# Splitting a first block's projections into high and low parts, with a new order of its stages

## The reference, cut to what matters

```python
# first block (hybrid_layer)
h = rms_norm(x, norm_g) * (1 + scale) + shift          # scale, shift, gate from silu(c) @ w_ada
proj = h @ w_in                                        # 1024 -> 2840 columns
q, kcr, vcr, ksl, vsl, kwn, vwn, z_a, g_br, u, z_s = split(proj)
q = rms_norm(q per head); k_slc, k_win likewise, then rope on q, k_slc, k_win
kc, vc = compress(kcr), compress(vcr)                  # gelu(blocks @ w1) @ w2
attn = nsa_attention(...) * silu(z_a)                  # compressed, selected and window branches
y = s5_mixer(u, ...)                                   # state space model, chunks of 8 tokens here
y = gelu(y); y = y * sigmoid(y @ glu_w + glu_b)
ssm = y * silu(z_s)
x = x + gate * (concat[attn, ssm] @ w_out)
# second block, two layers: rmsnorm, projections, two attentions, output projection (not changed)
```

## Time and profile before

| | us |
|---|---|
| median of 3 runs | 1032.58 (1031.73 to 1033.58) |
| profiled execution, its own time | 1031.98 |
| its span | 1030.1 |
| PE busy | 970.0 (94% of the span) |
| DVE busy | 578.7 (56%) |
| ACT busy | 428.1 (42%) |
| POOL busy | 86.3 (8%) |

### The profile page before, as it was taken

How to read it: one execution, slowest core, us unless ns; L and a number is a source line. 1 busy time by engine, 2 the same in 40 slices (tenths; PEclk the granted TensorE clock), 3 DMA queues, 4 the chain that set the end, 5 groups by cost and what they waited for, 6 DMA issues and landing times.

```text
span 1030.1 us, 13812 instructions
## 1 busy us (share of the span) xinstructions
PE 970.0 (94%) x5345; PEld 713.8 (69%) x5345; DVE 578.7 (56%) x1232; ACT 428.1 (42%) x936; POOL 86.3 (8%) x117
## 2 busy tenths in 40 slices
PE   3899999999898999999999998999999999998996
PEld 1446576744455677888678886788888678886784
DVE  2889499442589845533695244735333786234732
ACT  4221220123366733332592524833333592434821
POOL 1001310120008000000001000000000001000000
PEclk9899999999999999999899999999999899999998
DMA  9734157052460003343311533213333220433102
GB/s 361 280 116 92 54 76 245 1 164 82 163 165 1 2 21 106 121 126 100 93 59 42 143 92 97 101 54 111 97 103 100 80 98 24 126 100 123 63 1 82
DMA packets 81523, 104.64 MB, mean 102 GB/s; under 512 B 3745, under 2 KB 51921, under 8 KB 81442
## 3 DMA queue, kind: packets, MB, share of 16 engines
q1 hardware_dynamic: 75362, 81.24, 24.7%
q0 software_dynamic: 5808, 22.15, 7.8%
q10 hardware_dynamic: 288, 0.36, 0.1%
HBM read 98.37 MB, written 4.19 MB: 100 GB/s over the span
## 4 chain that ended last, share of the span: by engine, by line
PE 79%; DVE 8%; ACT 5%; DMA 3%; issue 3%; SPq 0%; DVEq 0%; POOL 0%; POOLq 0%; ACTq 0%; PEldq 0%
PE bank L883 74%; DVE ring L1781 2%; DMA ring<-in_w_in 2%; ACT ring L793 2%; PE bank L1130 1%; PE bank L1160 1%; DMA ring<-in_w_ada 1%; DMA ring<-in_cmp_w_v 1%; PE bank L1304 1%; DVE arena L1812 1%; DVE soft L1791 1%; DVE soft L1812 1%; ACT soft L800 1%; PE bank L1216 1%; ACT w_hi L743 0%
## 5 line engine op out<-in xcount | busy, mean ns | idle before, releaser
L1827 DVE TENSOR_TENSOR w_lo<-ring,w_hi 128x1024 fp32r<-128x1024 f32 x80 | 97.8, 1225 | 114.4 <-ACT w_hi L743 111.3
L883 PE MATMUL bank<-w_hi,hT_hi 128*128 128x512 f32 x320 | 125.3, 392 | 1.3 <-issue 1.0
L883 PE MATMUL bank<-hT_hi,w_hi 128*128 128x512 f32 x320 | 125.7, 393 | 0.0
L883 PE MATMUL bank<-w_lo,hT_hi 128*128 128x512 f32 x320 | 124.6, 389 | 0.0
L883 PE MATMUL bank<-hT_lo,w_hi 128*128 128x512 f32 x320 | 124.6, 389 | 0.0
L883 PE MATMUL bank<-hT_hi,w_lo 128*128 128x512 f32 x320 | 124.5, 389 | 0.0
L883 PE MATMUL bank<-w_hi,hT_lo 128*128 128x512 f32 x320 | 124.5, 389 | 0.0
L883 PE MATMUL bank<-hT_t,ring 128*128 128x512 f32 x224 | 100.1, 604 | 4.2 <-DMA ring<-in_w_in 3.6
L743 ACT ACTIVATE w_hi<-ring 128x1024 fp32r<-128x1024 f32 x80 | 84.4, 1058 | 11.6 <-PE bank L883 11.4
L883 PEld LDWEIGHTS bank<-hT_t,ring 128*128 128x128 f32 x224 | 42.5, 193 | 56.8 <-issue 53.1
L883 PEld LDWEIGHTS bank<-w_hi,hT_hi 128*128 128x128 f32 x320 | 60.1, 188 | 14.7 <-issue 2.6
(11 more groups left out here) (289 smaller groups left out, 1616.2 us busy)
## 6 DMA issues: line engine op xcount, KB each, us to landing
ring<-in_w_in SPq DMA_DIRECT2D x64, 512.0 KB, 4.5
ring<-in_w_ada SPq DMA_DIRECT2D x4, 2048.0 KB, 9.8
ring<-in_w_in SPq DMA_DIRECT2D x4, 2048.0 KB, 10.4
bias_ring<-in_na_bias POOLq DMA_DIRECT2D x8, 1024.0 KB, 5.3
ring<-in_w_out SPq DMA_DIRECT2D x16, 512.0 KB, 3.5
arena<-in_w_ada SPq DMA_DIRECT2D x2, 2048.0 KB, 19.4
ring<-in_w_out SPq DMA_DIRECT2D x2, 2048.0 KB, 13.1
bias_ring<-in_t_bias POOLq DMA_DIRECT2D x8, 448.0 KB, 3.7
```

Source lines behind the costliest of these rows:

```text
L883: return pe.matmul(out, lhsT, rhs, start=first, stop=last)
L1827: dve.tensor_tensor(w_lo[:, u % 4], raw_w[:, u % 4], w_hi[:, u % 4].bitcast(fp32), SUB).then_inc(S["w_split"], 1)
```

## The change

1. **Projections in three passes.** Every projection of the first block (U, KC, KV, KW, Q, ZS, ZA) becomes three float32r matmuls over high and low parts. `hT` is split into `x_hi` (ACT, 8 casts) and `hT_r` (DVE blocks 0 to 3, POOL blocks 4 to 7); DVE now applies scale and shift to all eight blocks. The weights are split in 24 parts: ACT makes every high part, DVE the low part 0, POOL the low parts 1 to 23. A part is 128x1024 (U, KC, ZS, ZA: one tile's weights; KV: half of them; Q: a quarter) or 128x560 (KW: a quarter).
2. **Order.** PE: U, KC, KV, KW, wt, kk, v, Q, W1, state products, ZS, ZA, GLU. DVE: after `cl_ready` the squares, scaling and turning of both kinds of keys for all four tiles at once (instructions of 512 and 256 elements), then the states, then queries two tiles at a time, then the hidden layer.
3. **Places and queues.** `toe` moves from `x_t` to three places and is filled by 24 DMAs; these and the DMAs of `u_dram` and `y_dram` are issued by SP between weight chunks. POOL zeroes the three places (one after `cl_ready`). `silu(z_a)` moves on DVE from the first turns of the pair loop to before the compressed softmax, and `ssm_out` moves four turns earlier. The first half of U's weights has a semaphore of its own.

```diff
+            def part_lo(n):                                   # POOL
+                pool.wait_ge(S["p_hi"], n + 1)
+                pool.tensor_tensor(p_lo(n), p_raw(n), p_hi(n).bitcast(fp32), SUB).then_inc(S["p_lo"], 1)
...
+            for k in range(4, KD):
+                pool.wait_ge(S["h_hi"], k + 1)
+                pool.tensor_tensor(hT_r[:, k, :], hT[:, k, :], x_hi[:, k, :].bitcast(fp32), SUB).then_inc(S["h_upper"], 1)
+            for n in range(1, 4):
+                part_lo(n)
+            settle(pool.memset(soft[:, 0:2048], 0.0))
+            settle(pool.memset(gate_b[:, :], 0.0))
+            for n in range(4, 12):
+                part_lo(n)
+            pool.wait_ge(S["cl_ready"], 1)
+            pool.memset(spent, 0.0).then_inc(S["zeroed"], 1)
+            part_lo(12)
+            pool.wait_ge(S["k_stats"], 1)
+            inv_root(HD, EPS, "k_rstd", lambda v: by_tile(v)[:, :, 8:12])
+            for n in range(13, 16):
+                part_lo(n)
+            for r in range(2):
+                pool.wait_ge(S["q_stats"], r + 1)
+                inv_root(HD, EPS, "q_rstd", lambda v: by_tile(v)[:, 2 * r:2 * r + 2, 0:8])
+            part_lo(16)
+            part_lo(17)
+            za_lo(0)
+            za_lo(1)
+            part_lo(18)
+            part_lo(19)
...
+            def proj_T(p, n):                                 # PE
                 if p >= 4:
                     pe.wait_ge(S["proj_evac"], p - 3)
+                part_ready(n)
+                for k in range(KD):
                     if p == 0:
                         pe.wait_ge(S["h_lower" if k < 4 else "h_upper"], k % 4 + 1)
+                    ins = mm3(bank[p % 4][:, :], (p_hi(n)[:, k, :], p_lo(n)[:, k, :]), (x_hi[:, k, :], hT_r[:, k, :]), k, k == 0, k == KD - 1)
...
+            for k in range(KD):                               # DVE
+                dve.tensor_scalar(hT[:, k, :], hT[:, k, :], modA[:, k:k + 1], modS[:, k:k + 1], MUL, ADD).then_inc(S["h_raw"], 1)
             for k in range(4):
-                dve.tensor_scalar(hT[:, k, :], ...).then_inc(S["h_lower"], 1)
+                if k == 1:
+                    dve.wait_ge(S["p_hi"], 1)
+                    dve.tensor_tensor(p_lo(0), p_raw(0), p_hi(0).bitcast(fp32), SUB).then_inc(S["u0_lo"], 1)
+                dve.wait_ge(S["h_hi"], k + 1)
+                dve.tensor_tensor(hT_r[:, k, :], hT[:, k, :], x_hi[:, k, :].bitcast(fp32), SUB).then_inc(S["h_lower"], 1)
...
+            for k in range(KD):                               # ACT
+                act.wait_ge(S["h_raw"], k + 1)
+                act.activation(x_hi[:, k, :], hT[:, k, :], ACT.Copy).then_inc(S["h_hi"], 1)
+                if k == 3:
+                    part_hi(0)
+            for n in range(1, 4):
+                part_hi(n)
             for f in range(4):
                 if f == 2:
                     act.wait_ge(S["ang_ready"], 1)
...
                 act.activation(cut(uT[:, f * T:(f + 1) * T], s=LC, n=NCH), src, ACT.Copy).then_inc(S["proj_evac"], 1)
+                part_hi(4 + f)
...
+                elif c == CH_W1:                              # SP
+                    sp.wait_ge(S["zeroed"], 2)
+                    sp.wait_ge(S["kk_evac"], 8)
+                    for g0, part in toe:
+                        for s in range(LC):
+                            sp.dma_start(part[s * SC:(s + 1) * SC, :, (LC - 1 - s) * SC:P],
+                                         kk[:, g0:g0 + part.shape[1], 0:(s + 1) * SC]).then_inc(S["toe_in"], 16)
```

More of the change, by code:

```diff
@@ L462, in _ @@
[L462 to L480, removed]
@@ L606, in _ @@
                 act.activation(q_tok[:, i, :], src[:, :], ACT.Copy).then_inc(S["proj_evac"], 1)
[L607 to L615, removed]
-                act.activation(dst, cut(bank[4 + n % 4][0:SC, :], a=4, m=P), ACT.Copy).then_inc(S["kk_evac"], 1)
             act.wait_ge(S["lam_dot"], 1)
             act.activation(lam_t, lam_t, ACT.Exp).then_inc(S["lam_exp"], 1)
-            for i in range(NT):
-                src = proj(PT_KW + i)
-                act.activation(kvw[:, i, :], src[:, 0:280], ACT.Copy).then_inc(S["proj_evac"], 1)
             for s in range(2):
@@ L624, in _ @@
                 act.activation(hid_tok[:, s * 256:(s + 1) * 256], bank[s][0:66, 0:256], ACT.Copy).then_inc(S["hid_evac"], 1)
+            part_hi(16)
+            part_hi(17)
+            for n in range(4):
+                act.wait_ge(S["y_done"], 4)
+                two, q = n % 2, n // 2
+                dst = u_in.rearrange("p (q a b) n -> p q a b n", q=2, b=2)[:, q, :, two, :]
+                act.activation(dst, cut(bank[4 + n][:, :], a=8, n=NCH), ACT.Copy).then_inc(S["y_evac"], 1)
+            za_hi(0)
+            za_hi(1)
             def move_zs(f):
@@ L1009, in _ @@
             ins.then_inc(S["hidT_done"], 1)
-            arrived(CH_ZS)
+            pe.wait_ge(S["toe_in"], 16 * LC * len(toe))
+            pe.wait_ge(S["state_ready"], 1)
+            st = cut(tmp_c, g=SG, n=NCH)
+            for n in range(4):
+                two, q = n % 2, n // 2
+                for a in range(8):
+                    g = 2 * (8 * q + a) + two
+                    w = NCH if a == 7 else 2 * NCH
+                    out = bank[4 + n][:, a * NCH:a * NCH + w]
+                    wide_ = lambda v: v.rearrange("p g n -> p (g n)")[:, g * NCH:g * NCH + w]
+                    mm(out, toe_of(g), wide_(u_in), True, False)
+                    ins = mm(out, cl3[:, g, SC:SC + P], wide_(st), False, True)
+                ins.then_inc(S["y_done"], 1)
             for f in range(4):
@@ L1014, in _ @@
                     pe.wait_ge(S["hid_ready"], 1)
[L1015 to L1031 removed]
+                proj_T(PT_ZS + f, 16 + f)
+                if f == 2:
                     pe.wait_ge(S["hid_gelu"], 1)
@@ L1217, in rows_T @@
                     ins.then_inc(S["xT_done"], 1)
-            def mm3(out, a, b, k, first, last):
-                mm(out, a[0], b[0], first, False)
-                mm(out, a[1], b[0], False, False)
-                return mm(out, a[0], b[1], False, last)
             def tile_T(out, l, g, f):
@@ new lines, in over_all, with squares, scale_heads @@
+            def over_all(v, n, h):
+                return v.unsqueeze(1).unsqueeze(1).to_broadcast([P, n, h, HD])
+            def squares(src, h, out, place):
+                sq = cut(place, i=src.shape[1], h=h, d=HD)
+                tt(sq, pairs_of(src, h), pairs_of(src, h), MUL)
+                return dve.tensor_reduce(out, sq, AX.X, ADD)
+            def scale_heads(src, h, r, g):
+                v = pairs_of(src, h)
+                tt(v, v, r.unsqueeze(3).to_broadcast([P, src.shape[1], h, HD]), MUL)
+                tt(v, v, over_all(row(g), src.shape[1], h), MUL)
```

410 lines of the change are left out of this document (243 added, 167 removed).

## The result

| | median us | runs | ratio to before, 95% interval |
|---|---|---|---|
| before | 1033.08 | 1031.73 to 1033.82 | |
| changed | 1051.92 | 1049.98 to 1053.0 | 1.0182 [1.0162, 1.0202] |

The change costs 19 us where 8 were forecast as a gain; the time is 10 us outside the range. The profiled execution has a span of 1048.2 us against 1030.1.

The account below looks back on a forecast made before the run. PE was taken to bound the kernel (79% of the chain). Its 33 us gain is waited away up to ZS's end; GLU 5.5 earlier plus pair loop 2.0 gives 7.5 off, median 1025.1 us, range 1011 to 1042.

Parts of the forecast that it names:

- Rows stand on both sides, so I take half.: DVE working beside POOL's low parts: it loses half of POOL's time, between a floor of nothing and all of it.
- rival A: DVE's two-input instructions wait for POOL's whole instruction, up to `cl_ready` and from `state_ready` to `hid_ready`: +16, 1040; chance 0.33.
- The row at 125.47: POOL's small scaling took 0.70 and ended just after DVE's two-input instruction; read as blocking in reverse.
- The scalings of the earlier trace: Two 128x384 DVE scalings took 2.49 us beside POOL's split of `w_out`, 0.87 after it; read as a full block.
- the toe blocks: `toe` filled after kk by 24 DMAs from SP: 15.4 us from kk's end kept, floor 10, ceiling 25.
- this rival: Low parts make PE wait tile by tile; dismissed as no rival, 2.37 us against 5.46, with no chance given.
- PE's gap ahead of kk: PE waits 18 us for `cl_ready` after wt, from 102.6 to 120.6.
- The clock behind a pause: PE's clock is low after the wait ahead of kk; kk takes 7.2 + 1.8 us.
- rival C: SP's 24 small DMAs for `toe` are slow, 10 us above the value taken: 1035; chance 0.07.
- The stall at ZS 2: PE at ZS tile 2 waits for `hid_ready`, which stands behind the queries on DVE: 2.9 us.
- PE's gain: Three float32r passes save 26.4 us on 18 tiles; with KV and KW, together 33 us.
- the halves: Half of POOL's time charged to DVE: 1.9, 6.5, 5, 2.4 and 5.9 us up to ZS tile 2.

Follow-up runs that it names:

- experiment 1: Changed kernel, but POOL makes none of the first block's low parts; PE takes the high part in their place: 1015.24 us, ratio 0.9817 to the kernel before.
- experiment 2: Kernel before with 16 idle 128x1024 POOL instructions, eight ahead of the u DMAs, eight behind: subtractions 1043.63 us, fills 1034.64, copies 1034.56.

## Why the prediction was wrong

**The step that failed: "Rows stand on both sides, so I take half."** DVE pays nearly all of POOL's 1.27 and 2.37 us, 0.87 by the two traces of experiment 1. By the prediction's own steps: the angles lose 16.7 us (6.5 taken, and 1.9 ahead of them, where DVE lost nothing); sines' end to `cl_ready`, 77.5 to 130.8, is 53.3 instead of 44.3, 9.0 of POOL's 10.3 (5 taken). `cl_ready` came at 130.8, forecast 120.6, rival A 131 to 134. From `state_ready` to `hid_ready` it took 36.2 us where 27.9 were written: six parts at 12.6 instead of five at 5.9, the rest a little more work of DVE's own.

The prediction weighed three rows and read one of them wrongly. DVE's instruction of 126.87 ran untouched inside POOL's 2.39 us root, but that root has 10 elements, so its length says nothing of how much it reads. It was no evidence on a subtraction that reads 1024 columns twice. It was not even a row without a clash: the same root took 1.95 us at 118.99, where DVE had next to nothing to do. The row at 125.47 has the new form on DVE's side alone, and there it was POOL that waited. The scalings of the earlier trace rows have it on POOL's side alone. No row had both, as the prediction says itself. Taking the mean of contrary rows was the error, as none of them measured the new work; experiment 2, sixteen idle subtractions in the kernel before, is what prices it.

The Trainium skill, page "SBUF — State Buffer", has GpSimd's reads, not its writes, contend with a two-input DVE instruction (section "Who interferes with whom"), and the later of the two block fully until the first ends (section "Summary: rules for kernel authors"). The subtractions (2.2 us lost of 2.37) and the fills (0 lost) agree; the copies (0.8 lost of 1.22) agree in kind and not in size. The prediction cited the rule and priced it as rival A, at 1040, and gave it 0.33; even that was 12 us short, for the reasons that follow.

**Where the late start of ZS tile 2 comes from.** It began at 223.0, forecast 202.1. Of these 20.9 us, 10.2 are `cl_ready`, 0.6 the clock behind kk's pause, 4.2 the toe blocks, and 8.3 the way from `state_ready` to `hid_ready`. The states gave 2.5 back: parts 14 and 15 fell at 152.0 and 157.6, where DVE was waiting for the toe blocks anyway, so they cost it nothing. Of the whole miss of 26.8 us this is most; the rest is named below.

**Further terms that were mis-sized.** The first tiles: KW and wt were to be done at 102.6 and were done at 112.7, since PE waited 4.3 us for low parts in U (the prediction dismissed this rival with 2.37 against 5.46, but POOL took 3.28 a part and four low blocks of `hT` came first) and ran at the lower clock around it (0.50 from 52 to 57). This is why PE's gap ahead of kk was 18.2, the forecast's 18, though both of its ends were 10 us late: one number that fits is no proof of the steps behind it. The clock behind a pause: kk lost 2.3, not 1.8; ZS 2 and 3 took 15.06 us where 12.2 was due, which had no term at all. The toe blocks: 19.6 us behind kk's evacuation, 15.4 taken, rival C's direction at less than half its size; the landing of 10.4 us in that sum was 2 on SP's queue, and the issues took 17.7 instead of 5. `state_ready` came at 186.8, forecast 174.2. The stall at ZS 2: 8.86, forecast 2.9.

**What held.** Float32r at 512 columns takes 0.232 us a matmul, at 256 0.118 and at 280 0.129, a little above the values taken (by these the 33 us of PE's gain are about 30, an estimate). The prediction's sums hold to within a microsecond: KW's end comes to 98.2 where it has 98.8, rival A's median to 1041 where it has 1040. The pair loop gave 1.5 of its 2.0: GLU is 19.0 later, the output projection 17.6 (403.94 against 386.39). The conditions for failure were named rightly: "if `state_ready` is past 185 the forecast is wrong at the halves". And with PE's 33 us less work and no low parts on POOL, experiment 1 came out 18.7 us faster than the kernel before.

## What to carry to other kernels

Before work goes to an engine that is 8% busy, look for which other engine it holds up: here POOL's 2.37 us cost DVE 2.2, while DVE would have done the same in 1.22. Price such a clash from a row in which both engines have the form of the new work. If there is none, put idle work of that form into the kernel as it is and measure it; a mean of rows of other forms is no price. When an engine is made faster, first look which slack it spends (25 us here) and refill the pause with work that waits for nothing, but check that a buffer's load then comes in time.

## What the runs showed that was not expected

- POOL's fills of 128x1024 leave DVE's two-input instructions alone (2.57 us each) but hold up its one-input scalings (128x16: 0.20 to 0.92 us).
- The cost is mutual: beside two-input DVE work POOL's subtraction of 1024 columns takes 4.07 us instead of 2.37, and tiny DVE instructions wait as long as large ones (one of 128x16 took 2.26 us, 0.18 alone).
- A POOL copy of 128x1024, 1.22 us beside small work, costs DVE 0.8.
- 24 small DMAs took SP 17.7 us to issue, and 12 of them 15.2 once POOL issued the other 12. The transfers themselves were short: 1.9 to 4.0 us from issue to landing in the changed kernel.
